# Input projection, latent norms and query projection of the attention layer as one stage, with the query products split into three float32r products

## What is computed

```python
def mla_project(h, pos, w_in, q_norm, kv_norm, w_qb, w_uk):
    z = h @ w_in                                        # 1024 -> 512 + 256 + 64
    q_a, c, kr = jnp.split(z, [Q_LORA, Q_LORA + KV_LORA], axis=-1)
    q = (rmsnorm(q_a, q_norm) @ w_qb).reshape(B, T, MLA_HEADS, NOPE_DIM + ROPE_DIM)   # 8 heads of 128 + 64
    q_nope, q_rope = q[..., :NOPE_DIM], q[..., NOPE_DIM:]
    q_lat = jnp.einsum('bthn,rhn->bhtr', q_nope, w_uk)  # 128 -> 256 for each head
    q_rope = rope(q_rope, pos).transpose(0, 2, 1, 3)
    c = rmsnorm(c, kv_norm)
    kr = rope(kr, pos)
    return q_lat, q_rope, c, kr
```

## Time and profile before

| | us |
|---|---|
| median of three runs | 2206.52 |
| lowest, highest | 2190.16, 2210.8 |
| the profiled execution | 2191.48 |
| its span, first to last instruction | 2189.8 |
| TensorE busy in it | 1992.3 |

### The profile page before, as it was taken

One profiled execution on the slowest core, in us unless ns is written; L12 is line 12 of the kernel. 1 busy time (PEld: TensorE's weight loads), 2 busy tenths in 40 slices (PEclk: granted clock), 3 DMA queues, 4 the chain that ended last, 5 costly groups with the idle time before them and its releaser, 6 DMA issues. The chain is left out here.

```text
span 2189.8 us, 51222 instructions
## 1 busy us (share of the span) xinstructions
PE 1992.3 (91%) x22040; PEld 1790.6 (82%) x22040; DVE 897.4 (41%) x1487; ACT 641.8 (29%) x1057; POOL 151.1 (7%) x199
## 2 busy tenths in 40 slices
PE   4789889998989999997799889999999899999995
PEld 4656556776989999996799759998855899999995
DVE  5323542223253333334655164454435443333334
ACT  3112434443142212222344333332212322212222
POOL 0001000431000000000400020000132000000000
PEclk7889999999999999998799989999979999999997
DMA  4012500875122232322122100001030222232221
GB/s 127 20 52 61 151 0 18 251 237 155 58 72 82 82 111 68 100 59 66 54 78 75 29 1 4 4 4 42 4 104 28 69 77 86 82 92 86 82 73 41
DMA packets 229241, 158.07 MB, mean 72 GB/s; under 512 B 12504, under 2 KB 221247, under 8 KB 228928
## 3 DMA queue, kind: packets, MB, share of 16 engines
q1 hardware_dynamic: 223412, 136.93, 21.1%
q0 software_dynamic: 5376, 18.36, 2.8%
q10 hardware_dynamic: 268, 0.08, 0.0%
HBM read 149.96 MB, written 5.34 MB: 71 GB/s over the span
## 5 line engine op out<-in xcount | busy, mean ns | idle before, releaser
L312 PE MATMUL ps<-ffn_xh,ffn_wh 128*128 128x280 f32 x1408 | 299.1, 294 | 18.0 <-DVE ffn_xl L1365 13.7
L312 PE MATMUL ps<-ffn_xh,ffn_wl 128*128 128x280 f32 x1408 | 297.2, 292 | 0.0
L312 PE MATMUL ps<-ffn_xl,ffn_wh 128*128 128x280 f32 x1408 | 296.1, 292 | 0.0
L312 PEld LDWEIGHTS ps<-ffn_xh,ffn_wh 128*128 128x128 f32 x1408 | 226.0, 190 | 19.0 <-issue 18.8
L312 PEld LDWEIGHTS ps<-ffn_xh,ffn_wl 128*128 128x128 f32 x1408 | 225.4, 190 | 0.0
L312 PEld LDWEIGHTS ps<-ffn_xl,ffn_wh 128*128 128x128 f32 x1408 | 224.6, 190 | 0.0
L1267 ACT CAST ffn_wh<-wa 128x1024 fp32r<-128x1024 f32 x88 | 91.3, 1041 | 208.1 <-PE ps L312 180.5
L312 PE MATMUL ps<-ffn_hid_h,ffn_wh 128*128 128x280 f32 x704 | 148.0, 291 | 0.0
L312 PE MATMUL ps<-ffn_hid_h,ffn_wl 128*128 128x280 f32 x704 | 147.6, 291 | 0.0
L312 PE MATMUL ps<-ffn_hid_l,ffn_wh 128*128 128x280 f32 x704 | 147.5, 291 | 0.0
L318 DVE TENSOR_TENSOR ffn_wl<-wa,ffn_wh 128x1024 fp32r<-128x1024 f32 x88 | 107.7, 1225 | 87.2 <-ACT ffn_wh L1267 87.2
(11 more groups left out here) (358 smaller groups left out, 3625.8 us busy)
## 6 DMA issues: line engine op xcount, KB each, us to landing
wa<-in_ffn_w_gate SPq DMA_DIRECT2D x44, 512.0 KB, 3.7
wa<-in_ffn_w_up SPq DMA_DIRECT2D x44, 512.0 KB, 3.7
arena<-in_cache SPq DMA_DIRECT2D x77, 160.0 KB, 3.4
wb<-in_ffn_w_down SPq DMA_DIRECT2D x16, 768.0 KB, 4.8
wb<-in_ffn_w_down SPq DMA_DIRECT2D x16, 640.0 KB, 4.3
arena<-in_cache POOLq DMA_DIRECT2D x63, 160.0 KB, 3.5
wb<-in_cache SPq DMA_DIRECT2D x40, 160.0 KB, 3.4
wb<-in_cache POOLq DMA_DIRECT2D x28, 160.0 KB, 3.6
```

What stands on the lines that cost most here:

```text
L312: mm = nc.tensor.matmul(dst[:, s, 0:HALF], a[:, c * width:(c + 1) * width], b[:, c, s * HALF:(s + 1) * HALF], start=first and n == 0, stop ...
```

## The change

The three blocks become one, with no meeting of the engines between them.

- The slabs of `w_in` are taken in another order: the four of the query latent, then the one of the rope key, then the two of the key latent. The squares of the query norm are taken as its slabs are kept, and its sum over the partitions is done behind the fifth slab.
- The rotation of the rope key, the key norm and the transposition of the keys are put between the products of the query projection: the sum of the key norm in the first pair of heads, tiles of keys in the pairs behind it. SyncE writes the keys out behind the last weight load.
- The query projection is no longer a hardware loop but four pairs written out. Every product is of the split kind. The 64 rope columns of both heads of a pair are put side by side and make one product of 128 columns; `cos` and `sin` are stored for 128 partitions, and VectorE rotates both heads together (`rope_pair`).
- The normed query latent, the weights of each pair, the transposed `w_uk` and the nope parts are cut into high and low parts by ScalarE and VectorE.

The core of the diff:

```diff
+                def project(i, bank, cols, first=False):
+                    for c in range(QC):
+                        if first and i == 0:
+                            pe.wait_ge(x_low, c + 1)
+                        mm = product(bank, wqh[:, i % 2, c, cols], wql[:, i % 2, c, cols], q_xh[:, c], q_xl[:, c], c == 0, c == QC - 1)
+                    return mm
...
+                def latents(i, u, c, free):
+
+                    pe.wait_ge(nope_low, 2 * i + u + 1)
+                    ge(pe, lat_kept, 4 * i + free)
+                    at = slice(u * KL + c * P, u * KL + (c + 1) * P)
+                    product(lat_bank[u, c], ukh[:, at], ukl[:, at], qnh[:, u], qnl[:, u], True, True).then_inc(lat_done, 1)
+
+                norm.tensor(pe)
+                for n in range(ZS):
+                    cut.multiply(pe, n, 0, DC, xh, xl, (z_low, 0) if n == 0 else None, z_cols[n])
+                    if n == ZROPE:
+                        norm_q.tensor(pe, 6)
+
+                for i in range(PAIRS):
...
+                    project(i, 4, slice(2 * NOPE, WQ), True).then_inc(q_rope, 1)
...
+                    project(i, 0, slice(0, NOPE)).then_inc(q_nope, 1)
+                    if i == 0:
+                        pe.wait_ge(uk_low, 1)
+                        norm_c.tensor(pe, 6)
+                    elif i == 1:
+                        pe.wait_ge(norm_c.done, RC)
+                        pe.wait_ge(zrope, 4)
+                        turn_keys(0)
+                    else:
+                        turn_keys(2 * i - 2)
+                    ge(pe, lat_kept, 4 * i)
+                    project(i, 2, slice(NOPE, 2 * NOPE)).then_inc(q_nope, 1)
+                    pe.wait_ge(uk_low, i + 1)
+                    latents(i, 0, 0, 0)
+                    pe.wait_ge(rope_read, i + 1)
+                    latents(i, 0, 1, 0)
+                    latents(i, 1, 0, 1)
+                    latents(i, 1, 1, 0)
+                    if i in (1, 2):
+                        turn_keys(2 * i - 1)
```

The order of VectorE behind the first two slabs, which the prediction follows:

```diff
+                for n in range(2, ZROPE + 2):
+                    cut.cut_low(dve, n, DC * z_cols[n])
+                dve.wait_ge(norm.done, DC)
+                norm_q.gather(dve)
+                cut.cut_low(dve, ZS - 1, DC * P)
+                cut_w(0, 0)
+                norm_q.invert(dve, 6)
+                cut_w(0, 1)
+                norm_q.scale(dve)
+                for c in range(QC):
+                    dve.wait_ge(x_high, c + 1)
+                    take_low(q_xl[:, c], hT[:, c], q_xh[:, c]).then_inc(x_low, 1)
+                rope_key()
+                dve.wait_ge(norm_q.done, QC)
+                norm_c.gather(dve)
+                for i in range(PAIRS):
+                    dve.wait_ge(uk_high, i + 1)
+                    take_low(ukl[:, :], ps[:, 6, 0:2 * KL], ukh[:, :]).then_inc(uk_low, 1)
+                    rope_pair(i)
+                    lower_nope(i, 0)
+                    if i == 0:
+                        norm_c.invert(dve, 6)
+                    elif i + 1 < PAIRS:
+                        cut_w(i + 1, 0)
+                    lower_nope(i, 1)
+                    if i == 0:
+                        cut_w(i + 1, 0)
+                    if i + 1 < PAIRS:
+                        cut_w(i + 1, 1)
+                    if i == 0:
+                        norm_c.scale(dve)
```

More of the change, by code:

```diff
@@ L296, in vector, with scale @@
                 self.invert(dve)
+                self.scale(dve)
+            def scale(self, dve):
                 dve.wait_ge(self.root, 1)
@@ L456, in program @@
         cut = Split("z", [w_turns[:, 0], w_turns[:, 1]], [w_turns[:, 2], w_turns[:, 3]], 0)
[L457 to L468, removed]
+        z_of = [0, 1, 2, 3, None, 4, 5]
@@ L479, in _ @@
[L479 to L512, removed]
@@ L600, in _ @@
[L600 to L606 removed]
+                    for u in range(2):
+                        pe.wait_ge(wa.used[u], wa.base[u] + turns[u] + i + 1 + FREE)
@@ new lines, in keep_latents, with keep_nope @@
+                def keep_latents(i, u, c):
+                    act.wait_ge(lat_done, 4 * i + 2 * u + c + 1)
+                    nc.scalar.copy(split(q[:, c, 2 * i + u]), halves(lat_bank[u, c])).then_inc(lat_kept, 1)
+                def keep_nope(i, u):
+                    act.wait_ge(q_nope, 2 * i + u + 1)
+                    nc.scalar.copy(split(qnh[:, u]), halves(2 * u)).then_inc(nope_high, 1)
+                norm.squares(act)
+                for n in range(2):
+                    cut.cut_high(act, n, 0, DC * P)
@@ L622, in _, with cut_w @@
             @block.vector
             def _(dve):
-                with dve.Fori(0, H // 2) as i:
-                    for u in range(2):
-                        h = i * 2 + u
-                        dve.wait_ge(wa.used[u], i + (wa.base[u] + 1) + FREE)
-                        rope(2, split(q[0:ROPE, 2, h]), roped, h * 4 + FREE)
-        for s in range(4):
-            wa.base[s] += H // 2
+                def cut_w(i, u):
+                    dve.wait_ge(w_high, 2 * i + u + 1)
+                    for dst, src in places(u):
+                        low = take_low(wql[:, i % 2, :, dst], raw_q(u)[:, :, src], wqh[:, i % 2, :, dst])
+                    low.then_inc(wa.used[u], 1)
@@ new lines, in _ @@
+                norm.gather(dve)
+                for n in range(2):
+                    cut.cut_low(dve, n, DC * P)
+                norm.vector(dve, gathered=True)
+                for c in range(DC):
+                    dve.wait_ge(z_high, c + 1)
+                    take_low(xl[:, c], hT[:, c], xh[:, c]).then_inc(z_low, 1)
+                for n in range(2, ZROPE + 2):
+                    cut.cut_low(dve, n, DC * z_cols[n])
+                dve.wait_ge(norm.done, DC)
+                norm_q.gather(dve)
@@ L632, in program @@
+        for u in range(4):
+            wa.base[u] += turns[u] + PAIRS
         if stop <= 1:
```

237 lines of the change are left out of this document (145 added, 92 removed).

## The result

The kernel after takes 2138.33 us (median of four runs: 2132.98, 2135.08, 2141.58, 2153.24), the kernel before, in four runs on the same chip, 2198.34 (2187.71 to 2210.8). The ratio is 0.975, with a 95% interval of 0.971 to 0.980. Forecast were 2145 us, 2130 to 2163, and faster.

The account below looks back on a forecast made before the run. TensorE was taken as bound by latency from 85.5 to 119.7 us, then by its products until 203.0. Prompt attention starting 53.75 us earlier gives 2138 us, or 2153 from a median-like run; halfway 2145, range 2130 to 2163.

Parts of the forecast that it names:

- Two bounds, one latency and one TensorE: Last slab to first query product, 34.2 us, is bound by latency; from there to the last latent, 83.3 us, by TensorE.
- Price of a product: In the query projection a split product costs 0.386 us against 0.50 plain; a pair 13.0 us without keys against 20.2.
- the 0.5 a pair kept for the range: Between second nope and head 1's latents: no loss taken, up to 0.5 us a pair allowed for the range.
- The chain through VectorE: VectorE's queue from last slab through first pair: query norm's reciprocal until 81.1 us, low part of nope 1 at 103.8.
- The waits: In the first pair TensorE waits for VectorE 0.9 us before head 0's latents and 3.6 before head 1's.
- The clock: Behind the first pair's 3.6 us wait TensorE falls to half clock; 2.5 us lost, 0 to 3.4 possible.
- The key writes: SyncE's key writes, now behind the loads, end at about 145 us, still before the last latents.
- The sum: Prompt attention starts at 150.65 us instead of 204.40, 53.75 less; what follows moves as a whole; execution 2138 us.
- The two kinds of runs: Whole executions fall two and two: 2138 us from the faster kind, 2153 from one like the median; 2145 halfway.
- VectorE as the bound in every pair: Rival, chance 0.10: the first pair's wait and clock loss come in the other three pairs too, 18 us, 2156 to 2163.
- The split products without their rate: Rival, chance 0.05: the query projection's 384 split products take 0.25 us each, 46.7 us more, 2192 us.
- Half clock for the whole query projection: Rival, chance 0.03: TensorE waits in each pair and stays at half clock, 27 us a pair, 2199 or 2206.5 us.

Follow-up runs that it names:

- experiment 4: The kernel after with its one stage cut into two blocks ahead of the first pair, so the engines meet there; one run, 2145.6 us.
- experiment 2: The kernel after with each pair's rope product done twice, 24 more float32r matmuls a pair; one run, 2144.7 us.
- experiment 1: The kernel after with one plain float32 product of the high parts in place of three float32r ones, cuts and waits kept; one run, 2152.5 us.
- experiment 3: The kernel after with the key norm's mean and reciprocal behind nope 1's low part and the next weight cuts, ScalarE's root behind the first pair's latents; one run, 2133.0 us.
- experiment 8: The kernel after with the key norm's sum and reciprocal at the second pair's end, scaling at the third's, all key tiles in the fourth; one run, 2134.3 us.
- experiment 10: Experiment 9 with ScalarE's key norm root moved behind the cast of w_uk and the third pair's weight cuts; median 2129.77 us, ratio 0.970 to the kernel before.
- experiment 7: The kernel after with three idle float32 products in the first pair's wait, ahead of head 1's latents; one run, 2133.1 us.
- experiment 5: The kernel after with two idle products in the gate stage's wait of 2.27 us; median 2129.96 us, ratio 0.972 to the kernel before.
- experiment 6: The kernel before with two idle products in the gate stage's wait of 2.27 us; median 2186.96 us, ratio 0.9985 to the kernel before.
- experiment 9: Experiment 8 with the two idle products of experiment 5 in the gate stage; median 2131.93 us, ratio 0.970 to the kernel before.

## Why the prediction was right, step by step

**Two bounds, one latency and one TensorE.** Right. The latency part is gone, but for 0.92 us; one meeting put back costs 5.6 (experiment 4), the rest is read from the rows; added TensorE work comes through at 11.6 of 12.3 us (experiment 2).

**Price of a product.** 0.77 us for six, as read from the slabs. A pair comes to 14.26 us rather than 14.0: 0.2 is TensorE standing between the first head's second latent and the second head's first (the product at 117.55 takes no more than 0.26, the next starts at 118.00), where the bank is still being copied out; the transposes took 0.41 us instead of 0.62, and some 0.3 I did not take apart. That lies inside the 0.5 a pair kept for the range. The last pair took 148.26 - 134.40 = 13.86 us against 13.5. From the first query product to the end of the last, TensorE's stretch shrank from 83.3 to 148.26 - 87.40 = 60.9 us. Of these 22.4 the split products give only 6.5 against plain ones in the same order (experiment 1); one rope product for two heads leaves out four stretches of 3.92 us, 15.7 at the plain price (11.6 at the split price, experiment 2).

**The chain through VectorE.** Every step stood in the predicted order, 0.2 us early at the query norm's reciprocal (80.86 against 81.1) and 1.1 early at the last low part (102.66 against 103.8): several operations start up to 0.1 us before the one ahead has ended in the rows (97.65 against 96.99 + 0.74), while a step was added for nearly each. ScalarE's wait for head 1's weights was there and ended at 79.75, against 80.1, released by the load of `w_qb`.

**The waits.** Of 0.9 + 3.6 us TensorE showed 0.2 and 3.06, released by what was named, with the reciprocal ahead of it. Experiments 3, 8 and 10 showed the cause as predicted, the order of the queue, and that it has two parts, which the prediction did not see: moving the reciprocal alone moves the wait to a later pair, where ScalarE's root stands in a queue as well.

**The clock.** 2.5 us taken, 1.7 measured, and 1.4 won back by filling the wait (experiment 7). In experiment 5's trace the same wait costs 1.2 us more than that, so the 2.5 lies between the two.

**The key writes.** The last one is issued by SyncE at 143.53, takes 0.42 and lands 1.5 us after its issue; the last latent's product ends at 148.26.

**The sum.** Start 149.28 against 150.65: waits 1.2 and clock 0.8 shorter, three later pairs 0.8 longer together without the clock's part, the handover at the end 0.2 shorter. These misses partly cancelled, which is luck, and left 1.4 us. What follows moved as a whole where the gate stage's clock was held, within some microseconds: the sum said 53.75, the stage's own gain is 55.12 in the two traces above and 202.59 - 148.79 = 53.80 in those of experiments 5 and 6, and from there to the end these two take 1979.9 and 1977.7 us. Their medians differ by 57.0, their profiled spans (2180.3 and 2128.7) by 51.6, so the runs can't say it more closely. In the profiled execution of the kernel after it did not move as a whole, for the gate stage's clock.

**The two kinds of runs.** Read rightly from the four executions before, but their cause was not looked for: the trace of before, a run of the faster kind, has the wait of 2.27 us and a granted clock of 0.87 behind it. Of the four runs after two are of the faster kind (2133 and 2135 us, where the sum gave 2138), one of the slower (2153, as the sum gave) and one lies between, so the median is 6.7 us under the 2145 put halfway. Which kinds came up in four runs is chance; the 2145 was a hedge and not a prediction of it.

**The rivals.** VectorE as the bound in every pair: one long wait in the first pair, 0.2 us in the others, and that behind ScalarE's copy. The split products without their rate: 0.77 for six. Half clock for the whole query projection: 3.4 us of it.

## What to carry to other kernels

When blocks are merged, the rows that show the waits say what latency there is to gain; what remains is the longest operation of a side engine that now stands in a shared queue. Moving it alone moves the wait (3.06 us in the first pair, then 1.96 in the second, 1.86 in the third); it goes, to 0.52, when what waits for that operation on the other engines' queues is moved behind what the main engine needs next. Where runs fall into two groups, look in the trace for a stage with a wait and a reduced clock behind it, and fill the wait before comparing small gains.

## What the runs showed of the hardware

The granted clock after a wait of about two microseconds is not settled by its length: 1.86 us in the same code halved it in one execution and not in another (experiments 8 and 9), 1.96 did not (experiment 3), 1.97 did, in another place with other work behind it. Nor is its return: behind the gate stage's wait of 2.27 us TensorE was busy for 40.03 of 40.92 us in the records and stayed at 0.51 throughout, while the same instructions before got back to 0.87 on average, and to 0.73 to 0.93 in six other traces. Two otherwise useless products there gave 1.00 in both kernels.
